# A decoder layer on one core: history, taps and y kept channel-major, and weights laid out slab by slab

## The reference, cut to what matters

```python
def conv_ffn(h, hist, w_up, conv_w, conv_b, w_down):
    T = h.shape[1]
    g_pre, u = jnp.split(h @ w_up, 2, axis=-1)            # 2048 -> 2 x 5632
    gp = jnp.concatenate([hist.astype(g_pre.dtype), g_pre], axis=1)
    conv = conv_b + conv_w[0] * gp[:, 0:T]
    for i in range(1, CONV_W):                            # width 3
        conv = conv + conv_w[i] * gp[:, i:i + T]
    y = (jax.nn.silu(conv) * u) @ w_down                  # 5632 -> 2048
    return y, gp[:, T:]                                   # the last two rows are an output

def layer(x, c, conv_hist, mix_a, mix_b, lw):
    mod = jax.nn.silu(c) @ w_ada + b_ada                  # 2048 -> 6 x 2048: shift, scale, gate, twice
    h = rmsnorm(x, norm1_g) * (1 + scale1) + shift1
    qa, ka, va, qb, kb, vb, r, log_a = project(h, w_in, ...)   # 2048 -> 6160
    x = x + gate1 * merge_out(mix_a(qa, ka, va), mix_b(qb, kb, vb, log_a), ...)  # w_out: 2048 -> 2048
    h2 = rmsnorm(x, norm2_g) * (1 + scale2) + shift2
    y, new_hist = conv_ffn(h2, conv_hist, w_up, conv_w, conv_b, w_down)
    return x + gate2 * y, ka, va, gla_state, new_hist
```

## Time and profile before

| | |
|---|---|
| median of 3 runs | 1593.41 us (1593.29 to 1593.66) |
| profiled execution | span 1592.4 us; the page gives no other time of it |
| PE busy | 1569.0 us (99%) |
| DVE, ACT, POOL busy | 899.9, 665.7 and 74.4 us |
| DMA | 371.06 MB in 239232 packets, 188371 of them under 2 KB |
| mean granted clock of PE | 0.995 |

### The profile page before, as it was taken

The page is one execution under the profiler, slowest core; times in us unless marked ns, Lnnn a source line. Parts: engine busy times, 40 slices in busy tenths (PEclk is TensorE's granted clock), DMA queues, the critical chain, the costliest instruction groups (busy, mean ns, idle before and its releaser), DMA issues.

```text
span 1592.4 us, 29203 instructions
## 1 busy us (share of the span) xinstructions
PE 1569.0 (99%) x12242; PEld 1418.5 (89%) x12242; DVE 899.9 (57%) x1525; ACT 665.7 (42%) x935; POOL 74.4 (5%) x131
## 2 busy tenths in 40 slices
PE   8999999999999999999999999999999999999997
PEld 4777888888888658888899999999999999999997
DVE  3555776656667536447454545545454566656663
ACT  3433444434446335325333333333333445545552
POOL 2000000001111000000000000000000000000000
PEclk8999999999999999999999999999999999999999
DMA  9999877777778998988844444454545554555460
GB/s 338 387 366 329 303 263 265 254 269 242 243 261 297 390 398 300 330 321 302 284 159 161 161 161 160 160 185 142 181 164 171 166 162 147 191 157 191 146 192 20
DMA packets 239232, 371.06 MB, mean 233 GB/s; under 512 B 7793, under 2 KB 188371, under 8 KB 230905
## 3 DMA queue, kind: packets, MB, share of 16 engines
q1 hardware_dynamic: 231888, 351.19, 63.8%
q0 software_dynamic: 7152, 17.90, 3.4%
q10 hardware_dynamic: 66, 0.14, 0.0%
HBM read 359.32 MB, written 9.88 MB: 232 GB/s over the span
## 4 chain that ended last, share of the span: by engine, by line
PE 84%; DMA 5%; issue 5%; DVE 3%; SPq 2%; ACT 2%; POOL 0%; ACTq 0%; POOLq 0%; DVEq 0%
PE ps L1046 24%; PE ps L1047 23%; PE ps L1048 23%; PE ps L998 3%; PE ps L1289 2%; DMA ring<-in_w_in 2%; PE ps L991 1%; DMA proj<-in_cache_v_win 1%; DMA vals<-in_w_ada 1%; SPq L610 1%; DMA ring<-in_w_out 1%; DVE wlo L2173 1%; PE ps L1360 1%; PE ps L1329 1%; ACT whi L1608 1%
## 5 line engine op out<-in xcount | busy, mean ns | idle before, releaser
L1046 PE MATMUL ps<-hhi,whi 128*128 128x288 f32 x3120 | 929.7, 298 | 1.5 <-DVE wlo L2014 0.5
L1047 PE MATMUL ps<-hlo,whi 128*128 128x288 f32 x3120 | 917.1, 294 | 0.0
L1048 PE MATMUL ps<-hhi,wlo 128*128 128x288 f32 x3120 | 917.0, 294 | 0.0
L1046 PEld LDWEIGHTS ps<-hhi,whi 128*128 128x128 f32 x3120 | 585.3, 188 | 43.6 <-issue 33.9
L1047 PEld LDWEIGHTS ps<-hlo,whi 128*128 128x128 f32 x3120 | 585.6, 188 | 0.7
L1048 PEld LDWEIGHTS ps<-hhi,wlo 128*128 128x128 f32 x3120 | 585.4, 188 | 0.0
L2014 DVE TENSOR_TENSOR wlo<-ring,whi 128x1024 fp32r<-128x1024 f32 x178 | 212.2, 1222 | 89.2 <-ACT whi L1599 88.8
L1599 ACT ACTIVATE whi<-ring 128x1024 fp32r<-128x1024 f32 x178 | 184.2, 1056 | 155.0 <-PE ps L1048 148.4
L2173 DVE TENSOR_TENSOR wlo<-ring,whi 128x1024 fp32r<-128x1024 f32 x96 | 117.0, 1222 | 84.6 <-ACT whi L1608 84.4
L1608 ACT ACTIVATE whi<-ring 128x1024 fp32r<-128x1024 f32 x96 | 100.8, 1053 | 145.6 <-PE ps L1048 112.3
L2695 DVE TENSOR_TENSOR wlo<-ring,whi 128x1024 fp32r<-128x1024 f32 (+1 forms) x94 | 105.7, 1132 | 56.0 <-ACT whi L1935 56.0
(11 more groups left out here) (323 smaller groups left out, 1141.5 us busy)
## 6 DMA issues: line engine op xcount, KB each, us to landing
ring<-in_w_up SPq DMA_DIRECT2D x88, 1024.0 KB, 5.2
ring<-in_w_ada SPq DMA_DIRECT2D x64, 1024.0 KB, 7.6
ring<-in_w_in SPq DMA_DIRECT2D x48, 1024.0 KB, 8.1
ring<-in_w_down SPq DMA_DIRECT2D x32, 1408.0 KB, 6.7
proj<-in_w_ada SPq DMA_DIRECT2D x28, 1024.0 KB, 9.4
ring<-in_w_out SPq DMA_DIRECT2D x16, 1024.0 KB, 8.6
ring<-in_cache_k_win SPq DMA_DIRECT2D x12, 1024.0 KB, 8.5
proj<-in_cache_v_win SPq DMA_DIRECT2D x8, 1024.0 KB, 13.1
```

The lines of the kernel that those rows point to most:

```text
L1046: mm(out, w_hi, x_hi, start=start, stop=False)
L1047: mm(out, w_hi, x_lo, start=False, stop=False)
L1048: return mm(out, w_lo, x_hi, start=False, stop=stop)
```

## The change

- The host lays w_in, w_out, w_up, w_down and the early slabs of w_ada out so that a slab is one block of HBM in which each partition's part is one run: 8 KB, for w_down 11 KB. The early slabs of w_in have a copy of their own, `w_in_early`. Size, order and destination of the loads are as before.
- `state_conv` comes channel-major from the host and is loaded once, 128 x 2816 bytes, into `history`; DVE copies from there into `gpad`.
- The taps of all 11 turns are gathered in `last_taps` and written with one DMA after the last turn, as a channel-major output that the host turns.
- y is one channel-major output. Each pair of tiles is written by POOL straight from `yst`. In the last turn the last chunk does tile 14 first and tile 15 then; ACT writes tile 14, SP tile 15.
- All transposes of history, taps and y are gone, with ACT's and DVE's copies of their results. The waits for the outputs at the end stand on SP.

```diff
+def column_blocks(w, rows, columns):
+    k, n = D // (P * rows), w.shape[1] // columns
+    return np.ascontiguousarray(w.reshape(k, rows, P, n, columns).transpose(3, 0, 2, 1, 4).reshape(n, k, P, rows * columns))
...
             def half_load(w, s, column, slot):
-                sp.dma_start(slab(slot, 8, 256), w[:, 8 * (s % 2):8 * (s % 2) + 8, bass.ds(column, 256)]
+                sp.dma_start(ring[:, slot, 0:2048], w[bass.ds(column, 1), s % 2].rearrange("a p c -> p (a c)")
                              ).then_inc(full[slot], 16)
...
-                    sp.dma_start(slab(s % SLOTS, 11, 256),
-                                 w_down[:, 11 * kg:11 * kg + 11, bass.ds(i * 512 + 256 * h, 256)]
+                    sp.dma_start(ring[:, s % SLOTS, :], w_down[bass.ds(i * 2 + h, 1), kg].rearrange("a p c -> p (a c)")
                                  ).then_inc(full[s % SLOTS], 16)
-            sp.wait_ge(first_row_out, 1)
-            sp.dma_start(o["y_p"][0:P, 1536:2048], yrow[0]).then_inc(y_end_out, 16)
+            sp.wait_ge(*DE.upto("u", 0))
+            sp.dma_start(o["y"][:, 15], yst[:, 3]).then_inc(last_odd_out, 16)
+            for s, n in ((conv_out, 16), (k_out, 256), (v_out, 256), (stp_out, 64), (s0_out, 128), (y_out[0], 64),
+                         (y_out[1], 48), (last_even_out, 16), (last_odd_out, 16)):
+                sp.wait_ge(s, n)
...
             pool.wait_ge(*OL.upto("l3"))
-            pool.dma_start(hrow[:, 0], hist[:, 0:512]).then_inc(hist_in[0], 16)
...
+            pool.dma_start(history.rearrange("p n b r -> p (n b r)"), a["state_conv"].rearrange("p n c -> p (n c)")
+                           ).then_inc(hist_in, 16)
+            pool.wait_ge(*FV.upto("last", 10))
+            pool.dma_start(o["new_conv"], last_taps).then_inc(conv_out, 16)
+            for i in range(4):
+                for h in range(2 if i < 3 else 1):
+                    pool.wait_ge(*DV_.upto(f"u{h}", i))
+                    pool.dma_start(o["y"][:, 4 * i + 2 * h:4 * i + 2 * h + 2], yst[:, 2 * h:2 * h + 2]
+                                   ).then_inc(y_out[h], 16)
...
-                for n in range(4):
-                    last = turn(ps[:, 4, 16 * n:16 * n + 16], hrow[:, par, P * n:P * n + P], ident[0:16, 0:16])
...
-                for n in range(4):
-                    last = turn(ps[0:18, 5, P * n:P * n + P], glast[:, n, :], ident)
...
+            act.wait_ge(*DV_.upto("u1", 3))
+            act.dma_start(o["y"][:, 14], yst[:, 2]).then_inc(last_even_out, 16)
...
-                dve.wait_ge(*FT.upto("hist", i))
+                dve.wait_ge(hist_in, 16)
...
                 def out(h):
                     dve.wait_ge(used, i * 24 + (CH_DOWN + BUFS + 21 + 3 * h))
-                    dve.wait_ge(*DT.upto("t2", i - 1))
+                    if i:
+                        dve.wait_ge(y_out[h], 16 * i)
...
+                def last_out():
+                    dve.wait_ge(y_out[1], 48)
+                    dve.wait_ge(last_even_done, 1)
+                    dve.wait_ge(*DV_.upto("u0", 3))
+                    gated(5 * KD, 14, ps[:, 2:3, :], lambda m: yst[:, 2, :], DV_, 1, 3)
+                    dve.wait_ge(used, 3 * 24 + (CH_DOWN + BUFS + 24))
+                    dve.wait_ge(*DV_.upto("u1", 3))
+                    gated(5 * KD, 15, ps[:, 3:4, :], lambda m: yst[:, 3, :], DE, 0, 0)
```

More of the change, by code:

```diff
@@ L328, in build @@
         conv_out = sem("conv_rows_out")
-        y_out = sem("y_rows_out")
-        kv_stored, conv_stored = (sem(f"{n}_stored") for n in ("kv_rows", "conv_rows"))
+        y_out = [sem(f"y_tiles_out{h}") for h in range(2)]
+        kv_stored = sem("kv_rows_stored")
         s0_in, s0_out = sem("state_in"), sem("state_out")
-        hist_in = [sem(f"history_in{j}") for j in range(2)]
+        hist_in = sem("history_in")
         st = lambda name, *names: Steps(sem(name), *names)
@@ L777, in _ @@
                 ask(which)
-            columns = [0, D_FF, 256, D_FF + 256]
+            half = D_FF // 256
+            columns = [0, half, 1, half + 1]
             for s in (0, 2):
@@ L793, in _ @@
             half_load(w_up, 7, columns[3], 3)
-            columns = [512, D_FF + 512, 768, D_FF + 768]
+            columns = [2, half + 2, 3, half + 3]
             half_loads(w_up, columns, CH_UP + 16, range(0, 1))
@@ L1919, in up_turn @@
                     his(16, 18)
-                act.wait_ge(*FT.upto("rows", i))
-                act.wait_ge(conv_stored, i + 1)
-                f(crows, ps[0:18, 5, :], ACT.Copy).then_inc(*FA.step("rows"))
             for i in range(11):
@@ L2544, in _, with gated @@
             head_lo(1)
-            def gated(gate, tile, psum, out, steps, n, i, end=False):
-                tmp = tmp_s[:, 64 * (n % 2):64 * (n % 2) + 64]
-                ts = tmp.rearrange("p (n b t) -> p n b t", n=2, b=NB)
-                gs = modT[:, bass.ds(tile + gate, 2), 1:NC9].rearrange("p n (b a) -> p n b a", a=1)
+            def gated(gate, tile, psum, out, steps, n, i):
+                c = psum.shape[1]
+                tmp = tmp_s[:, 64 * (n % 2):64 * (n % 2) + NS * c]
+                ts = tmp.rearrange("p (n b t) -> p n b t", n=c, b=NB)
+                gs = modT[:, bass.ds(tile + gate, c), 1:NC9].rearrange("p n (b a) -> p n b a", a=1)
+                first, last_step = (f"s{n}", f"u{n}") if steps is not DE else ("s", "u")
                 v.tensor_tensor(ts, psum[:, :, SEQ:TOK].rearrange("p n (b t) -> p n b t", t=TS),
-                                gs.to_broadcast([P, 2, NB, TS]), ALU.mult).then_inc(*steps.step(f"s{n}"))
-                for m in range(2):
-                    last = v.scalar_tensor_tensor(
+                                gs.to_broadcast([P, c, NB, TS]), ALU.mult).then_inc(*steps.step(first))
+                for m in range(c):
+                    v.scalar_tensor_tensor(
                         out=out(m)[:, 0:SEQ], in0=psum[:, m, 0:SEQ],
@@ L2558, in gated @@
                         op0=ALU.mult, op1=ALU.add)
-                if end:
-                    last.then_inc(last_shown, 1)
-                dve.wait_ge(*steps.upto(f"s{n}", i))
-                for m in range(2):
+                dve.wait_ge(*steps.upto(first, i))
+                for m in range(c):
                     last = v.tensor_tensor(out(m)[:, SEQ:TOK], tmp[:, NS * m:NS * m + NS],
                                            xT[:, bass.ds(tile + m, 1), SEQ:TOK].rearrange("p a c -> p (a c)"), ALU.add)
-                last.then_inc(*steps.step(f"u{n}"))
+                last.then_inc(*steps.step(last_step))
             def out_tiles(n):
@@ L2739 @@
     tables, gates = constants(), gate_tables(inputs["w_in"], inputs["w_gate2"])
+    laid = {"tables": tables, "gates": gates, "state_conv": channel_tiles(inputs["state_conv"]),
+            **weight_slabs(*(inputs[n] for n in ("w_in", "w_out", "w_up", "w_down", "w_ada")))}
     arrays, a, o = {}, {}, {}
-    for name, x in {**inputs, "tables": tables, "gates": gates}.items():
+    for name, x in {**inputs, **laid}.items():
         x = np.ascontiguousarray(x)
```

194 lines of the change are left out of this document (58 added, 136 removed).

## The result

The median is 1569.64 us (1568.85 to 1570.76, four runs) against 1593.41: a ratio of 0.985, 95% interval 0.984 to 0.987. The forecast was 1569.9. The profiled execution took 1570.0 us with a span of 1568.1; before's span was 1592.4, so 24.3 us went. I split them by counting TensorE's matmuls of the split products (the three-pass ones) in both traces, which are the same in number and order, and reading when the same one starts.

The account below looks back on a forecast made before the run. TensorE's instruction list and the two ends were taken to bound the kernel. 15.4 + 6.8 + 1.0 + 0.3 = 23.5 us off the 1592.4 us span gives 1568.9, plus 1.0 around it 1569.9 us; forecast range 1567.5 to 1572.5 (0.62).

Parts of the forecast that it names:

- TensorE's list: TensorE's instructions between first weights and last matmul: each one removed saves its slot, 15.4 us in all.
- the tail: Behind the last matmul: less work, an earlier landing and GpSimd's closing out of the way; 6.8 us gained, 2.6 to 7.4.
- the start: First modulation slabs: longer runs shorten TensorE's waits, slower table loads cost some; 1.0 us gained, between -0.5 and 2.0.
- Transposes in the up-projection: History and tap transposes between turns leave TensorE: 0.99 us ten times, plus first and last turn, 10.7 us.
- Transposes of y: Twelve per block of 512 columns, three times, 4.0 us, and six between the last two chunks, 0.7 us.
- Cover: DVE and ACT don't need the time TensorE's stops gave them; the new waits on DVE cost nothing.
- GpSimd's own closing: The unnamed 4.7 us at the span's end are GpSimd's; they start earlier once its last DMA is earlier.
- closing stays: Rival: the 4.7 us at the end remain, 4.2 us of the tail's gain go, 1574.1 us; chance 0.13.
- The term for the tables: At the start, GpSimd's 720 KB of tables land 1 to 2 us later beside 8 KB runs; 0.8 us counted as loss.
- The middle: Between 480 and 600 us, where cache loads bound a few places: 0.3 us gained, between -0.7 and 2.
- Small transfers lose: Rival: w_in's 8 KB packets delay small loads, TensorE stalls at perhaps four places, no start gain; about 1575 us, chance 0.12.
- starving rival: Rival: state loads wait for a long packet each time, 19 us on each of three heads; 1628 us, chance 0.03.

Follow-up runs that it names:

- slots_back: Changed kernel with dummy transposes of constants at the old places in TensorE's list, no copies, DMAs or waits; 1585.33 us, ratio 0.9947.
- layout_only: Kernel before with only the weights laid out slab by slab in long runs; 1591.30 us, ratio 0.9987.
- waits_on_pool: Changed kernel with the final waits for all outputs moved from SP back to GpSimd; 1571.10 us, ratio 0.9859.
- vectors_late: Changed kernel with the norm vectors transposed four x tiles later, after tile 11 instead of 7; 1569.61 us, ratio 0.9846.
- after_again: Changed kernel measured once more, unaltered, beside later runs on one chip; 1568.64 us, ratio 0.9844.
- after: The changed kernel in its first measurement, against the kernel before; 1569.64 us, ratio 0.985.
- late_w_in_old: Changed kernel with only the 28 later slabs of w_in in their old 1 KB runs; 1568.86 us, ratio 0.9845.
- early_old: Changed kernel with only the early slabs of w_ada and w_in in their old 2 KB runs; 1570.01 us, ratio 0.9852.
- old_runs: Changed kernel with the weights in their old layout, runs of 1, 2 and 8 KB; 1572.23 us, ratio 0.9873.
- before_waits_on_sp: Kernel before with the final waits moved from GpSimd to SP, GpSimd still issuing a DMA at the end; 1591.06 us, ratio 0.9984.

## Why the prediction was right

The forecast of the median is 0.26 us off, which is better than its terms are. TensorE's list was 0.6 us too high and the tail 0.6 too low, the start 0.7 too high, and the stretches between the start and the first turn gave 1.9 us where 0.3 was forecast. Together 24.3 us went from the span, not 23.5; and around the span of the changed kernel's profiled run lie 1.9 us (1570.0 less 1568.1), where 1.0 was taken. That these cancel is luck; that transposes and tail make the gain is not.

*Transposes in the up-projection, 10.7 forecast.* Right: 0.98 us for each of ten turns, where 0.99 was said, taps behind the last turn 0.44 for 0.45. Only the first turn's four were free: that term, 0.34, was put in although TensorE had a wait there. Real: 10.2 to 10.3. slots_back shows that it was TensorE's slots and nothing beside them; that the 33 small DMAs and ScalarE's copies cost nothing holds too, since D comes back to 0.02 us without them.

*Transposes of y, 4.7 forecast.* 1.31 for each of three groups (1.33 said), 0.66 for the six (0.7). Real: 4.6. D gained 14.8 us of the 15.4 forecast for the list. C's 0.5 us is not the transposes': layout_only, which has them all, shows it too (156.99 against 157.46).

*Cover.* VectorE and ScalarE did not need the stops: the half turn without transposes takes 25.28 us in both kernels. The new waits cost nothing: slots_back has them, and its D is that of the kernel before to 0.02 us.

*The tail, 6.8 forecast, 7.4 measured.* The mis-sized term is the way to the landing, 2.55 us for 3.0: VectorE's half took 0.7 as said, but the DMA of 144 KB landed in 1.8, not 2.1, and the handovers were shorter. SP's closing was 0.4 for 0.5. The reading of the earlier trace rows as GpSimd's own closing holds in its main point: it runs beside the work when GpSimd's last DMA is early, and nothing like it shows on SP. It was wrong in that the length is no constant 4.7 us: the DRAIN took 4.40 us before and 3.23 beside the work in the changed kernel, and waits_on_pool ends 2.1 us behind the landing. The rival "closing stays" is out.

*The start, 1.0 forecast, 0.26 in this profile.* The signs of both terms were right: TensorE's waits for slabs (0.38 and 1.60) went, tables need 10.4 to 10.6 us in place of 8.1. The term for the tables, 0.8, was counted rightly: vectors_late waits 1.11 us for them, and in after_again TensorE gets to the bias products just as they land. What the prediction put at nothing is the clock. In the profile of `after` it was at its lower level from 15.5 to 29.1 us, in after_again from 16.7 to 26.9, and the bias products came at 34.05 instead of 33.08; that is the whole difference of their P0. It arises in the products of the first slabs, where neither waits: 6.09 us in `after`, 5.03 in after_again. The wait for the norm vectors at 16 us, 0.85, had not been foreseen either, but moving it (vectors_late) left P0 at after_again's. Over the kernels, long early runs give 0.5 to 0.8 us at P0 and 0.3 behind it, so 1.0 was close for the sum; a single profile can't show it.

In 15 to 25 us the changed kernel, with 8 KB runs, moves 415 and 424 GB/s (windows above), the kernel before, with 2 KB runs, 385 and 388: the rate went up with the runs. The Trainium skill, "DMA: Bandwidth & Descriptors", section "Where 436 GB/s comes from", has the HBM side, about 358 GB/s, bind such transfers. Both kernels' traces are above that.

*The middle, 0.3 forecast, 1.1 measured between 444 and 578 us.* Its 1.1 us in this profile lie between 444 and 473 us, while the prediction had looked for its 0.3 between 480 and 600; what frees them stays open (late_w_in_old, above). Over the whole of B other waits come on top. B is 132.7 to 133.7 in all but three kernels, whatever their edits, and 134.1 in before, 134.8 in vectors_late, 136.4 in slots_back. In the last two the clock was halved for a stretch behind waits for cached values, which the kernels have near 570 us (1.4 to 1.5 us, in some a second one of up to 0.6). Windows of slots_back:

```profile
566.00:572.00 6.00, 4.49 (x48) 1.20 (x40) 0.57 (x1) 0.04 (x1) 0.00 (x0) 1.00 1.02 418
572.00:578.00 6.00, 5.71 (x27) 2.65 (x28) 0.29 (x1) 1.19 (x2) 0.00 (x0) 0.56 1.02 417
```

Before keeps its full clock there. early_old, old_runs and before_waits_on_sp vary as the long-run kernels do, so the change as such need not be behind it.

*Small transfers lose, and starve.* The first is real at the start, at about 1 us (the wait of 1.11 in vectors_late). In 200 to 490 us it isn't. TensorE's waits there in the changed kernel (us in total, times, longest) are all on VectorE:

```profile
PE ps L1174 <- DVE proj L2256: 0.9, 3, 0.4
PE ps L1243 <- DVE proj L2281: 0.2, 1, 0.2
```

The starving rival would have been 19 us a head; A would show it, and A got shorter. The eight loads of states, whose packets are of 1 KB, land in 4.6 to 9.0 us, 5.5 at the median, where they took 4.2 to 8.9 and 6.6 before. What 8 KB runs were seen to hold up are loads at the start, that of the tables most, by 2.5 us.

## What to carry to other kernels

Where TensorE never idles, count its slots: an instruction taken off its list is worth its distance to the next one plus what it does to its neighbour (eight small transposes 0.98 us, twelve of 128 x 128 1.31), unless TensorE stands in front of a wait, as the first history transposes did; dummy instructions put back at the same places test this for one run. Let GpSimd have its last DMA and its last wait some microseconds before the end, so that its DRAIN (1.6 to 5.0 us here) runs beside the work, and leave the last transfers and the final waits to another engine. Longer runs for hidden weight loads are worth nothing, and for the loads that the start hangs on about a microsecond, part of which the small transfers beside them give back.

## What the runs showed of the hardware that I had not expected

- GpSimd's closing is one DRAIN behind its last instruction: 4.40 us (before), 5.00 (before_waits_on_sp, begun with its last DMA), 1.62 (waits_on_pool), 3.23 (after, begun with its last DMA and hidden). The timeline doesn't list it, the view of its source line does. SP's took 0.007 us in the changed kernel, where the span ended 0.4 us behind the last landing.
- The 720 KB of tables took 8.0 to 8.3 us beside 2 KB runs and 10.4 to 10.6 beside 8 KB runs in the kernels named above.
- A half clock can be cheaper than the work that averts it: x tiles at a granted clock of 0.50 took 0.87 us each; with one filler product of 256 columns each, at 1.00, they took 1.03.
- The same program's first split product started at 45.33 and 44.36 us in two executions (after, after_again). Both have the same 0.8 us wait of TensorE near 16 us; the clock fell to its lower level (1.2 GHz, a granted clock of 0.50) at 15.5 us and stayed there to 29.1 in one, from 16.7 to 26.9 in the other.
